# Two transformer blocks on one core: memory attention by whole heads, with its four heads staggered between the query units and the output units

## What is computed

```python
def memory_attention(h, mem_h, wq, wk, wv, wo):
    b, s, _ = h.shape
    q = (h @ wq).reshape(b, s, MEM_HEADS, MEM_HEAD_DIM)
    k = (mem_h @ wk).reshape(b, -1, MEM_HEADS, MEM_HEAD_DIM)
    v = (mem_h @ wv).reshape(b, -1, MEM_HEADS, MEM_HEAD_DIM)
    sc = jnp.einsum("bqhd,bkhd->bhqk", q, k).astype(jnp.float32) * (MEM_HEAD_DIM ** -0.5)
    p = jax.nn.softmax(sc, axis=-1).astype(v.dtype)
    o = jnp.einsum("bhqk,bkhd->bqhd", p, v).reshape(b, s, D_MODEL)
    return o @ wo
```

## Time and profile before

| | |
|---|---|
| median of 3 runs | 1050.96 us (1050.93 to 1051.23) |
| the profiled execution | 1051.46 us, of which the span is 1049.7 us |
| PE busy | 990.9 us, 94% of the span |
| DVE, ACT, POOL busy | 617.8, 514.1 and 74.6 us |
| mean granted TensorE clock | 0.986 |
| chain that ended last | PE 84%, DVE 8%, ACT 5% |

### The profile page before, as it was taken

The page is one execution under the profiler, slowest core; times in us unless marked ns, Lnnn a source line. Parts: engine busy times, 40 slices in busy tenths (PEclk is TensorE's granted clock), DMA queues, the critical chain, the costliest instruction groups (busy, mean ns, idle before and its releaser), DMA issues.

```text
span 1049.7 us, 13392 instructions
## 1 busy us (share of the span) xinstructions
PE 990.9 (94%) x5001; PEld 830.4 (79%) x5001; DVE 617.8 (59%) x761; ACT 514.1 (49%) x734; POOL 74.6 (7%) x100
## 2 busy tenths in 40 slices
PE   6999999899999999999988898989998899999996
PEld 5888888688788888877876677978997678888884
DVE  4555445764755455456776584655653556666765
ACT  5544443565564443445554265425442356465653
POOL 2300000000100000000005251100000000000000
PEclk9999999999999999999999898999999999999999
DMA  8865655441455655554344051224552424646441
GB/s 283 263 195 190 197 178 185 160 180 41 161 186 195 192 180 187 200 200 159 113 168 140 3 186 56 81 92 149 201 199 82 130 101 162 209 159 201 168 152 41
DMA packets 106777, 166.01 MB, mean 158 GB/s; under 512 B 5676, under 2 KB 79692, under 8 KB 106604
## 3 DMA queue, kind: packets, MB, share of 16 engines
q1 hardware_dynamic: 104640, 160.39, 45.8%
q0 software_dynamic: 1936, 5.00, 1.6%
q10 hardware_dynamic: 160, 0.07, 0.0%
HBM read 164.38 MB, written 1.05 MB: 158 GB/s over the span
## 4 chain that ended last, share of the span: by engine, by line
PE 84%; DVE 8%; ACT 5%; issue 1%; DMA 1%; POOL 0%; POOLq 0%; ACTq 0%; SPq 0%; DVEq 0%
PE ps L1700 24%; PE ps L1702 24%; PE ps L1701 24%; DVE w_lo L1143 2%; DVE arena L1587 2%; PE ps L1998 2%; PE ps L1966 1%; ACT w_hi L576 1%; PE ps L1893 1%; PE ps L1900 1%; ACT xT_hi L631 1%; PE ps L2241 1%; PE ps L1724 1%; PE ps L1970 1%; PE ps L2227 1%
## 5 line engine op out<-in xcount | busy, mean ns | idle before, releaser
L1143 DVE TENSOR_TENSOR w_lo<-raw,w_hi 128x2048 fp32r<-128x2048 f32 (+2 forms) x143 | 327.9, 2303 | 176.9 <-ACT w_hi L576 176.7
L1700 PE MATMUL ps<-w_hi,xT_hi 128*128 128x512 f32 (+2 forms) x898 | 348.9, 389 | 13.9 <-DVE w_lo L1149 3.2
L1702 PE MATMUL ps<-w_hi,xT_lo 128*128 128x512 f32 (+2 forms) x898 | 341.9, 381 | 0.0
L1701 PE MATMUL ps<-w_lo,xT_hi 128*128 128x512 f32 (+2 forms) x898 | 341.4, 380 | 0.0
L576 ACT ACTIVATE w_hi<-raw 128x2048 fp32r<-128x2048 f32 (+2 forms) x143 | 269.8, 1898 | 96.0 <-PE ps L1702 81.9
L1700 PEld LDWEIGHTS ps<-w_hi,xT_hi 128*128 128x128 f32 x898 | 170.6, 190 | 47.6 <-issue 9.2
L1702 PEld LDWEIGHTS ps<-w_hi,xT_lo 128*128 128x128 f32 x898 | 170.3, 190 | 32.6
L1701 PEld LDWEIGHTS ps<-w_lo,xT_hi 128*128 128x128 f32 x898 | 170.6, 190 | 29.9
L1700 PE MATMUL ps<-w_hi,hT_hi 128*128 128x512 f32 x232 | 90.9, 392 | 1.8 <-DVE hT_lo L1277 1.8
L1702 PE MATMUL ps<-w_hi,hT_lo 128*128 128x512 f32 x232 | 90.5, 390 | 0.0
L1701 PE MATMUL ps<-w_lo,hT_hi 128*128 128x512 f32 x232 | 90.3, 389 | 0.0
(11 more groups left out here) (273 smaller groups left out, 1033.6 us busy)
## 6 DMA issues: line engine op xcount, KB each, us to landing
raw<-in_ffn_w_gu SPq DMA_DIRECT2D x88, 512.0 KB, 4.8
raw<-in_ffn_w_down SPq DMA_DIRECT2D x44, 512.0 KB, 3.9
raw<-in_w_ffn_up SPq DMA_DIRECT2D x44, 512.0 KB, 5.4
raw<-in_w_in SPq DMA_DIRECT2D x38, 512.0 KB, 4.6
raw<-in_w_out SPq DMA_DIRECT2D x24, 512.0 KB, 4.2
raw<-in_w_ffn_down SPq DMA_DIRECT2D x22, 512.0 KB, 4.2
raw<-in_w_mem_k SPq DMA_DIRECT2D x8, 512.0 KB, 4.4
raw<-in_w_mem_v SPq DMA_DIRECT2D x8, 512.0 KB, 4.6
```

What stands on the lines that cost most here:

```text
L1143: TTn(w_lo[HOME[k]][:, 0:n], raw[k % RING][:, 0:n], w_hi[HOME[k]][:, 0:n].bitcast(F32), ALU.subtract).then_inc(resid, 1)
L1700: pe.matmul(out_, lh, rh, start=first, stop=False, **kw)
L1701: pe.matmul(out_, lh, rl, start=False, stop=False, **kw)
L1702: return pe.matmul(out_, ll, rh, start=False, stop=last, **kw)
```

## The change

The query weights come in another cut: unit i of `mq` holds all eight row tiles of the 256 columns of head i, so after each unit one head's queries are complete. The four heads are then handled one by one, and their steps are put between the query units and the halves of the output units. Groups, `norm("mo")` and `to_1024` go away; each head's result is transposed (`mem_turn_out`) and split as soon as it is there, and output unit i waits for head i alone. The number of matmuls, transposes and bytes stays.

```diff
@@ SP @@
-            two_row_tiles("mq", a["w_mem_q_2"][0])
+            for i in range(4):
+                k = U0["mq"] + i
+                load(k, rows_by_cols(k, a["w_mem_q_2"][0], 0, 8, 256 * i, 256))
@@ ACT @@
-            dense("mq", 4)
-            act.wait_ge(unit_used, END["mq"])
-            act.activation(qT3[:, 0:4, :].rearrange("p a b -> p (a b)"), banks(0, 2), ACT.Copy).then_inc(m3_act, 1)
-            attention(4, 2)
-            norm("mo")
-            dense("mo", 4)
+            def mem_q(h):
+                act.wait_ge(unit_used, U0["mq"] + h + 1)
+                act.activation(qT3[:, 2 * h:2 * h + 2, :].rearrange("p a b -> p (a b)"), ps[:, MEM_Q_BANK[h], :],
+                               ACT.Copy).then_inc(q3_ready, 1)
+            def mem_exps(h):
+                act.wait_ge(neg3_ready, h + 1)
+                if h >= 2:
+                    act.wait_ge(pT3_ps, h - 1)
...
+            def mem_out_hi(h):
+                act.wait_ge(o3T_ps, h + 1)
...
+            split(u + 2)
+            mem_q(0)
+            split(u + 3)
+            mem_q(1)
+            split(v)
+            mem_exps(0)
+            mem_q(2)
+            split(v + 1)
+            mem_exps(1)
+            mem_q(3)
+            mem_out_hi(0)
+            mem_exps(2)
+            mem_exps(3)
+            mem_out_hi(1)
+            split(v + 2)
+            mem_out_hi(2)
+            split(v + 3)
+            mem_out_hi(3)
+            split(v + 4)
+            split(v + 5)
@@ DVE (mem_max, mem_pT, mem_out, mem_out_lo are row maximum, copy of the turned probabilities, result, lo half) @@
+            split(u + 2)
+            split(u + 3)
+            mem_max(0)
+            split(v)
+            mem_pT(0)
+            mem_max(1)
+            mem_out(0)
+            split(v + 1)
+            mem_pT(1)
+            mem_max(2)
+            mem_out_lo(0)
+            mem_out(1)
+            mem_max(3)
+            mem_pT(2)
+            mem_out_lo(1)
+            mem_out(2)
+            mem_pT(3)
+            split(v + 2)
+            mem_out(3)
+            mem_out_lo(2)
+            split(v + 3)
+            mem_out_lo(3)
+            split(v + 4)
+            split(v + 5)
@@ PE @@
+            def mem_scores(h):
+                pe.wait_ge(q3_ready, h + 1)
+                if h:
+                    pe.wait_ge(p3_ready, h)
+                for t in range(TT):
+                    for d in range(2):
+                        last = pe.matmul(ps[:, 2, t * S:t * S + S], qT3[:, 2 * h + d, t * P:t * P + P],
+                                         kT3[:, 2 * h + d, :], start=(d == 0), stop=(d == 1))
+                last.then_inc(sc3_ps, 1)
...
+            def mem_late(h):
+                mem_weighted(h)
+                mem_turn_out(h - 1)
+            mem_q(0)
+            mem_q(1)
+            mem_scores(0)
+            mem_q(2)
+            mem_turn(0)
+            mem_scores(1)
+            mem_weighted(0)
+            mem_q(3)
+            mem_turn(1)
+            mem_scores(2)
+            mem_turn_out(0)
+            mem_weighted(1)
+            mem_scores(3)
+            mem_turn(2)
+            by_rows("mo", 0, lambda: mem_late(2))
+            mem_turn(3)
+            by_rows("mo", 1, lambda: mem_late(3))
+            mem_turn_out(3)
+            by_rows("mo", 2)
+            by_rows("mo", 3)
```

More of the change, by code:

```diff
@@ L96 @@
 SLOT0 = {"wp": 4}
-GROUPS = [("mla", g, (1, 2), 4, MV) for g in range(4)] + [("mem", g, (2, 2), 2, MEMD) for g in range(2)]
+GROUPS = [("mla", g, (1, 2), 4, MV) for g in range(4)]
+MEM_Q_BANK = (0, 1, 4, 5)
 WINDOWS = [(0, (0, 1, 2, 3)), (0, (4, 5, 6, 7)), (1, (0, 1)), (1, (2, 3)), (1, (4, 5)), (1, (6, 7))]
@@ L749, in exps @@
                 kind, g, nk, hg, dv = GROUPS[gi]
[L750 removed]
+                scale = QK ** -0.5
                 at = 0
@@ L768, in attention @@
                     exps(gi)
-                    if GROUPS[gi][0] == "mla":
-                        split(U0["out_ssd"] + gi - first + 2)
+                    split(U0["out_ssd"] + gi - first + 2)
                     if gi == 2:
@@ L1397, in attention @@
                     attn_out(gi)
-                    if GROUPS[gi][0] == "mla":
-                        side_add(gi - first)
-                        split(U0["out_ssd"] + gi - first + 2)
+                    side_add(gi - first)
+                    split(U0["out_ssd"] + gi - first + 2)
                     if gi == 2:
@@ L1964, in scores @@
                         out_ = banks(0, 3)[:, at + h * n:at + h * n + n]
[L1965 to L1971, removed]
+                        last = pe.matmul(out_, qT2[0:QK + 2, head, t * P:t * P + P], kT2[0:QK + 2, head, keys],
+                                         start=True, stop=True)
                     last.then_inc(sc_ps, 1)
@@ L2318, in _, with mem_q @@
                 norm("mq", 2 * i, 2)
-            turned_result("mq")
-            pe.wait_ge(m_act, 1)
-            pe.wait_ge(m_dve, 1)
-            pe.wait_ge(m3_act, 2)
-            pe.wait_ge(m3_dve, 2)
-            attention(4, 2)
-            pe.wait_ge(o_ready, 6)
-            norm("mo")
-            to_1024("mo")
+            def mem_q(h):
+                k = U0["mq"] + h
+                if h == 2:
+                    pe.wait_ge(m_act, 1)
+                pe.wait_ge(resid, k + 1)
+                for r in range(KT):
+                    if h == 0:
+                        xT_there("mq", r // 2 * 2 + 1)
+                    for j in range(2):
+                        last = product(ps[:, MEM_Q_BANK[h], j * S:j * S + S], wt(k, 256 * r + P * j, P),
+                                       (xT_hi[:, r, :], xT_lo[:, r, :]), r == 0 and j == 0, r == KT - 1,
+                                       skip_group_check=True)
+                last.then_inc(unit_used, 1)
@@ new lines, in mem_weighted @@
+            def mem_weighted(h):
+                pe.wait_ge(pT3_ready, h + 1)
+                if h == 0:
+                    pe.wait_ge(m_act, 1)
+                    pe.wait_ge(m_dve, 1)
+                else:
+                    pe.wait_ge(o3_ready, h)
+                for t in range(TT):
+                    for kt in range(TT):
+                        at = (t * TT + kt) * P
+                        last = pe.matmul(ps[:, 0, t * S:t * S + S], probT3[h % 2][:, at:at + P],
+                                         v3[:, kt, h * MEMD:h * MEMD + MEMD], start=(kt == 0), stop=(kt == 1))
+                last.then_inc(o3_ps, 1)
@@ new lines, in mem_turn_out @@
+            def mem_turn_out(h):
+                pe.wait_ge(o3_ready, h + 1)
+                if h:
+                    pe.wait_ge(o3_lo, h)
+                for j in range(2):
+                    for t in range(TT):
+                        last = pe.transpose(ps[:, 1, j * S + t * P:j * S + t * P + P],
+                                            o3[:, t, h * MEMD + j * P:h * MEMD + j * P + P], ident)
+                last.then_inc(o3T_ps, 1)
+            def mem_late(h):
+                mem_weighted(h)
+                mem_turn_out(h - 1)
```

91 lines of the change are left out of this document (60 added, 31 removed).

## The result

The changed kernel takes 1040.63 us (median of 4 runs, 1039.65 to 1041.18); the kernel before, on the same chip, 1051.1 us (4 runs, 1050.93 to 1051.47). The ratio is 0.990, 95% interval 0.9888 to 0.9914. The profiled execution took 1041.18 us, 10.28 less than that of before.

A forecast was written before the change was run, and what follows sets the result against it. PE's work plus its gaps was taken to bound the kernel. The attention's 9.67 us gap, less 0.7 for seams and 0.1 for one wait, gave 8.9 us: 1051.46 to 1042.6, 1042.1 on the median's scale; range 1040.8 to 1044.8.

The forecast's parts named there:

- What bounds it: Whole kernel: PE busy 990.9 of 1049.7 us; no matmul goes away, so only the attention's 9.67 us gap can be won.
- Cover: Memory attention: recurring hand-overs of 0.82 to 2.15 us hide under PE work between, except one wait of 0.1 us.
- Rival A: Stagger hides only part: hand-overs 0.5 to 1 us longer lose 1.8 to 7.8 us; 1043.9 to 1049.9 us, chance 0.12.
- Rival B: No gain: every head still exposes its softmax, 8.6 us or more returns, time within 0.2% of before; chance 0.03.
- Splits and loads: Weight splits (ACT 1.9, DVE 2.29 us) hidden under output units, query loads land in time: no cost.
- rival C: Slower: alternating short groups bring PE to 1.2 GHz for 11.0 us of work; 1053 us or more, chance 0.03.
- The sum: Whole stage: gap 9.67 less seams 0.7 less one wait 0.1 gives 8.9 us gained.
- Scores and weighted values: Attention: eight fp32 matmuls take 3.56 us, twice for scores and twice for weighted values, 7.12 us each.
- Transposes: Attention: 32 transposes, eight more costing 0.93 us by printed durations, 3.72 us in all.
- Seams: PE's new list: 23 changes between unlike groups at 0.03 us each, 0.7 us; bounds 0 to 1.8 us.
- Output product: Product behind the attention, 823.29 to 845.45: 22.16 us of PE work, unchanged.
- The one wait: Scores of head 3: ACT's copy of the turned result stands before head 2's exps, so 0.1 us of wait returns.

The follow-up runs named there:

- experiment 1: Changed kernel without the stagger: single heads, all four query units before them and all four output units behind; 1048.97 us.
- experiment 2: Changed kernel with heads staggered among the query units only, all heads ended before the first output unit; 1046.68 us.
- experiment 4: Changed kernel with ACT's split of output unit 1 moved between the copy of head 0's turned result and head 2's exps; 1041.76 us.
- experiment 5: Changed kernel with groups of four transposes strewn singly between products in the out_mla and value units ahead of the stage; 1043.67 us.
- experiment 6: Changed kernel with transposes strewn singly between products in the value units only; 1043.03 us in one execution.
- experiment 3: Changed kernel with ACT's exps of head 2 ahead of its copy of head 0's turned result; 1040.53 us.
- experiment 7: Changed kernel with transposes of inputs turned as a whole done by column tile instead of by token tile; 1039.48 us.
- experiment 9: Kernel of experiment 8 with DVE's split of unit out_mla+1 moved behind the conversions of the turned values; 1039.23 us.
- experiment 8: Kernel of experiment 7 with scores of head 3 and turns of head 2 behind the first half of output unit 0; 1040.23 us.
- experiment 10: Changed kernel with only DVE's split of unit out_mla+1 moved behind the conversions, transposes still by token tile; 1040.05 us.

## Why the prediction was right, and where it was off

**What bounds it, and that gaps are all there is to win: right.** PE's busy time is unchanged and all of the gain is inside the stage.

**Cover: right, at every place named.** No wait of the six came back. Experiments 1 and 2 take the cover away and get 7.64 and 4.86 us back where 7.2 and about 4.5 were expected, and experiment 4 pays 1.80 for a split of 1.90 put into the tightest place. Rival A needed every hand-over to be 0.5 us longer or more, and scores to probabilities took the 2.15 us of the forecast (803.46 to 805.61); its wait of 1.4 us at the scores of head 3 does not come out of its own terms, 2.15 + 0.5 against 2.24. Rival B needed no cover at all, and even heads without the stagger cover 2.6 us.

**Splits and loads, put at no cost: right.** PE waits for neither within the stage, and the feed-forward begins as before, 0.54 us of wait included in both kernels' 1.57 us between 835.22 and 836.79.

**The clock (rival C): it did not come.** The granted clock is 1.00 in the stage in all kernels of this study, those with waits of 1.57 us among their short groups too. The Trainium skill, in TensorE: Matmul & The Clock Gate, A second HAM failure mode: psum-queue depth-cycling, would have led to expect it for groups that cycle through PSUM banks with small idles between them. The changed kernel has the cycling without the idles, experiments 1 and 2 have both, and their traces, with 1.00, do not agree. The prediction's "once in this trace" was wrong beside that: in the kernel before the clock is also granted at about 0.9 from 540 to 660 us, and at 0.80 in the last 12.6 us.

**The sum: its size failed, by 1.4 us.** The forecast stage, from the first query matmul on, was 72.90 - 8.87 = 64.03 us; it measured 62.64 (772.58 to 835.22), which is nearly all of the 1.5 us between the forecast 1042.1 and the measured 1040.63. The step that failed is "PE's work stays at 23.11 + 17.96 + 22.16": the 17.96 was read from groups that had just come out of a wait, and from printed durations. By terms:

- Scores and weighted values, put at 14.24 us (four times 3.56 for two groups each). In running work eight groups of 1.73 take 13.84: 0.40 less. Experiments 1 and 2 show where it comes from: weighted values take 1.83 behind a wait and 1.73 otherwise, and the pairs that the prediction read hold one of either, 3.56.
- Transposes, put at 3.72 from a difference of two printed durations. By starts eight groups of about 0.435 take 3.48: 0.24 less.
- Seams, put at 0.03 each, 0.69 in all. The scores at 784.17 show the balance: 1.54 us to the next product instead of 1.73, and then 0.30 instead of 0.12, 0.01 less in sum. The prediction had read the same balance at transposes (0.20 instead of 0.12, and 0.35 ahead of it, which is less than 0.43 by as much) and still took a price. Where transposes stand between products, experiments 5 and 6 give 0.010. In this stage it is nearly nothing, 0.69 less. By the Trainium skill, in TensorE: Matmul & The Clock Gate, Step-by-step, a seam would be free; the trace agrees within that 0.01, and by it the forecast would have been 0.7 us nearer.
- Output product, put at 22.16: 62.64 - 23.11 - 13.84 - 3.48 - 0.20 leaves 22.01 for it, 0.15 less. Of this 0.08 is a wait again: in the kernel before, the first matmul behind the 0.97 us took 0.31 us to the next start, the others 0.23.
- The one wait, put at 0.1: 0.13, and 0.07 in the group behind it. Its size was nearly right and its cause was not (experiment 3). The prediction ended the hand-over at ACT's last sum, 2.15 us, and left out the 0.14 until PE starts (805.61 to 805.75); with it the hand-over is 2.29 and no longer covered.

These are 0.40 + 0.24 + 0.69 + 0.15 - 0.10 = 1.38 us, the 1.39 by which the stage beat the forecast. The four larger errors had one sign, and the range's low end allowed only for the seams: "seams and the wait at nothing", a gain of 9.7, capped by a gap of 9.67. The gap itself was taken too small, since the cost of coming out of a wait was counted as work and transposes by their printed durations. With 1.73 and 0.435 in the sum the gap of before is 27.63 - 13.84 - 3.48 = 10.3 us, and the stage gained 10.26.

## What to carry to other kernels

Price work that is to run without gaps from a distance between starts in the middle of running work, never from a group that begins behind a wait and never from a printed duration; what a wait costs beyond its idle time belongs to the gap. Cover is worked out hand-over by hand-over, end of the producing matmul to start of the next, against the work laid between, and an engine's list matters only if the operation ahead ends later than the operand comes. When a wait will not move, look at what the engine it names was doing just before: in experiment 7 that was a split that nobody needed yet.

## What the runs showed of the hardware that I had not expected

**Coming out of a wait costs PE more than the idle time printed.** A group of four fp32 matmuls of 256 columns takes 0.10 us more behind waits of 1.15 and 1.57 us (weighted values, experiment 1), and 0.07 more behind waits of 0.13 and 1.76 (scores, changed kernel and experiment 4), so the surplus did not grow with the wait. Two waits printed as 1.56 us cost 2.08 by starts (experiment 5).

**The time of these kernels spreads outside the stage, in stretches where the clock is granted below 1.** From 190 us behind the first feed-forward product on, the granted clock and PE's busy time for the same work differ between the changed kernel (first row) and experiment 1 (second):

```profile
1026.79:1040.79 14.00, 4.50 (x20) 3.38 (x18) 5.47 (x8) 2.30 (x4) 2.09 (x2) 0.79 0.18 75
```

```profile
1034.26:1048.26 14.00, 6.18 (x21) 4.56 (x19) 5.47 (x8) 2.30 (x4) 2.08 (x2) 0.74 0.18 75
```

DVE and ACT are busy for as long in both. The changed kernel's program ends at 1039.4, so 1.4 us of its row are empty; up to 1039.3 the clock is 0.83. From the first feed-forward product to the end the first took 202.6 us and the second 204.2; experiments 6 and 9 took 204.3, and all the others 202.6 to 202.8. Ahead of the stage the transposes of `out_mla` start at 698.47 us in experiment 8 and at 695.15 in experiment 9, though PE's list up to there is the same in both, and at 698.59 in experiment 10, which has the same moved split as 9; between 540 and 660 us the clock is granted at about 0.9 with places that differ. What makes these stretches fall one way or the other was not found, and it is why the small edits here were judged by the stage's own length.
